# Strassen-style MLP of a two-layer streaming encoder: one block of down weights moved to other buffers, a tile of transposes moved, VectorE and ScalarE orders rewritten

## The reference

```
h = rms_norm(x, norm_mix);  proj = h @ w_in                  # q, k, v, u, gv
x = x + concat(window_attention(q, k, v, sinks), u * spatial_gating(gv)) @ w_o
h = rms_norm(x, norm_ffn)
x = x + square(relu(h @ w_up)) @ w_down                      # 1024 -> 4096 -> 1024
```

## Time and profile before

| | us |
|---|---|
| time, 3 runs: lowest, median, highest | 994.88, 997.0, 997.27 |
| the profiled execution's own time | 992.74 |
| its span, first to last instruction | 990.8 |
| PE busy (share of span) | 943.6 (95%) |
| DVE busy | 707.6 (71%) |
| ACT busy | 562.7 (57%) |
| POOL busy | 204.8 (21%) |

### The profile page before, as it was taken

The page is one execution under the profiler, slowest core; times in us unless marked ns, Lnnn a source line. Parts: engine busy times, 40 slices in busy tenths (PEclk is TensorE's granted clock), DMA queues, the critical chain, the costliest instruction groups (busy, mean ns, idle before and its releaser), DMA issues.

```text
span 990.8 us, 14055 instructions
## 1 busy us (share of the span) xinstructions
PE 943.6 (95%) x5632; PEld 828.1 (84%) x5632; DVE 707.6 (71%) x813; ACT 562.7 (57%) x843; POOL 204.8 (21%) x136
## 2 busy tenths in 40 slices
PE   8999998998999999999799999988989989998995
PEld 5888787987997998898688888888879879988984
DVE  5676436888787878868647761487876977878785
ACT  5556427674665574476455661657546735745753
POOL 2554223110110011001147424401101101100110
PEclk9999999999999999999899999989989999999998
DMA  8432050776577568474534213236838565775653
GB/s 292 136 103 84 22 170 1 192 153 208 140 170 204 133 177 204 121 215 85 190 102 160 78 62 83 87 85 173 193 105 236 122 192 135 168 207 128 173 105 128
DMA packets 40497, 141.76 MB, mean 143 GB/s; under 512 B 5616, under 2 KB 5744, under 8 KB 40432
## 3 DMA queue, kind: packets, MB, share of 16 engines
q1 hardware_dynamic: 28624, 98.32, 29.2%
q0 software_dynamic: 11520, 41.95, 23.9%
q10 hardware_dynamic: 288, 0.59, 0.2%
HBM read 138.74 MB, written 2.10 MB: 142 GB/s over the span
## 4 chain that ended last, share of the span: by engine, by line
PE 57%; DVE 19%; DMA 13%; ACT 5%; issue 5%; POOL 1%; SPq 0%; DVEq 0%; POOLq 0%; ACTq 0%
DMA raw<-weights_in 12%; PE bank L579 10%; PE bank L581 10%; PE bank L580 10%; DVE wlo L1289 9%; PE bank L576 7%; PE bank L578 7%; PE bank L577 7%; DVE flo L1553 3%; ACT whi L932 2%; DVE xt L1586 2%; DVE raw L1566 2%; PE bank L603 1%; PE bank L777 1%; DMA xt<-x_in 1%
## 5 line engine op out<-in xcount | busy, mean ns | idle before, releaser
L932 ACT ACTIVATE whi<-raw 128x1024 fp32r<-128x1024 f32 x268 | 279.5, 1056 | 174.4 <-DMA raw<-weights_in 88.5
L1289 DVE TENSOR_TENSOR wlo<-raw,whi 128x1024 fp32r<-128x1024 f32 x218 | 264.0, 1222 | 108.8 <-ACT whi L932 108.6
L579 PE MATMUL bank<-xhi,wlo 128*128 128x256 f32 (+1 forms) x672 | 211.2, 314 | 11.4 <-issue 8.9
L581 PE MATMUL bank<-xlo,whi 128*128 128x256 f32 (+1 forms) x672 | 209.2, 311 | 0.0
L580 PE MATMUL bank<-xhi,whi 128*128 128x256 f32 (+1 forms) x672 | 209.0, 311 | 0.0
L576 PE MATMUL bank<-wlo,fhi 128*128 128x512 f32 x448 | 179.2, 400 | 23.6 <-DVE xt L1586 20.1
L548 POOL DMA_DIRECT2D raw<-weights_in x80 | 69.4, 868 | 539.6 <-DVE raw L1566 333.1
L577 PE MATMUL bank<-whi,fhi 128*128 128x512 f32 x448 | 177.6, 396 | 0.0
L578 PE MATMUL bank<-whi,flo 128*128 128x512 f32 x448 | 177.5, 396 | 0.0
L535 POOL TENSOR_TENSOR wlo<-raw,whi 128x1024 fp32r<-128x1024 f32 x50 | 135.2, 2716 | 203.4 <-ACT whi L932 203.4
L579 PEld LDWEIGHTS bank<-xhi,wlo 128*128 128x128 f32 x672 | 130.4, 194 | 19.0 <-issue 12.5
(11 more groups left out here) (131 smaller groups left out, 1240.7 us busy)
## 6 DMA issues: line engine op xcount, KB each, us to landing
raw<-weights_in SPq DMA_DIRECT2D x172, 512.0 KB, 4.5
raw<-weights_in POOLq DMA_DIRECT2D x80, 512.0 KB, 6.2
xt<-x_in SPq DMA_DIRECT2D x4, 512.0 KB, 8.2
gbc<-gains_in SPq DMA_DIRECT2D x4, 512.0 KB, 4.5
out_t<-xt SPq DMA_DIRECT2D x3, 512.0 KB, 2.7
gbc<-gains_in ACTq DMA_DIRECT2D x1, 512.0 KB, 5.8
bias<-alibi_in SPq DMA_DIRECT2D x2, 256.0 KB, 7.3
wst<-ws_in SPq DMA_DIRECT2D x2, 256.0 KB, 6.9
```

Source lines behind the costliest of these rows:

```text
L579: pe.matmul(o, wlo[:, s, wc], hi[:, tokens], start=first, stop=False, skip_group_check=on_sum)
L581: return pe.matmul(o, whi[:, s, wc], lo[:, tokens], start=False, stop=last, skip_group_check=on_sum)
L932: act.activation(whi[:, n % SLOTS, :], raw_at(slot), ACT.Copy).then_inc(whi_ready, 1)
L1289: dve.tensor_tensor(wlo[:, n % SLOTS, :], raw_at(raw_slot(n)), whi[:, n % SLOTS, :], ALU.subtract) \
```

## The change

Four things change. First, the down phase's B22 for M3 goes into slots 2 and 3, when M4's lows are made, and no longer into M2's slots 4 and 5; the next quarter's M7, which also uses 2 and 3, is therefore loaded behind the lows of the down phase's M3, and stands last in SP's list. Second, M4's weight sum in the down phase is made by DVE from M2's block in slots 4 and 5, as in the up phase, and POOL's accumulating DMA for it goes. Third, the last tile of x is turned before the last quarter of product M1, not behind it. Fourth, the orders on DVE and ACT are new, in q0's up phase and in all down phases. The waits and counts follow. The diff, without the counting functions and the q > 0 branch of the up orders (which keeps its order):

```diff
@@ -71,11 +71,12 @@
 RAW_SLOTS = 6
 B11, B12, B21, B22 = range(4)
-PRODUCT_SLOT = (0, 4, 4, 2, 0, 2, 2)
+PRODUCT_SLOT = ((0, 4, 4, 2, 0, 2, 2), (0, 4, 2, 2, 0, 2, 2))
 PRODUCT_BLOCK = {M1: B11, M2: B21, M3: B22, M7: B22}
...
@@ -444,23 +443,24 @@
                 if pos >= 4:
                     wait_low(sp, nth(l, pos - 4))
                 elif l:
-                    wait_low(sp, nth(l - 1, group_pos(QUARTERS - 1, DOWN, M4 if pos < 2 else M5, pos % 2)))
+                    wait_low(sp, nth(l - 1, group_pos(QUARTERS - 1, DOWN, M3 if pos < 2 else M5, pos % 2)))
                 load(l * LAYER_ROWS + pos, mix_slot(pos))
             def load_block(l, q, ph, r, g):
-                before = divmod(phase(l, q, ph) - 1 - l * 2 * QUARTERS, 2)
                 if r == M3:
-                    wait_low(sp, nth(l, group_pos(q, ph, M2, g)))
+                    wait_low(sp, nth(l, group_pos(q, ph, M2 if ph == UP else M4, g)))
                     if ph == UP:
                         sp.wait_ge(weights_summed, summed_weights(l, q, UP, M4, g))
-                elif q or ph:
-                    wait_low(sp, nth(l, group_pos(*before, {M1: M5, M7: M4, M2: M3}[r], g)))
+                elif ph == DOWN:
+                    wait_low(sp, nth(l, group_pos(q, UP, {M1: M5, M7: M4, M2: M3}[r], g)))
+                elif q:
+                    wait_low(sp, nth(l, group_pos(q - 1, DOWN, {M1: M5, M7: M3, M2: M2}[r], g)))
                 elif r != M2:
-                    wait_low(sp, nth(l, MLP_POS - 4 + PRODUCT_SLOT[r] + g))
+                    wait_low(sp, nth(l, MLP_POS - 4 + PRODUCT_SLOT[UP][r] + g))
                 elif l:
-                    wait_low(sp, nth(l - 1, group_pos(QUARTERS - 1, DOWN, M3, g)))
-                load(block_row(l, q, ph, PRODUCT_BLOCK[r], g), PRODUCT_SLOT[r] + g)
+                    wait_low(sp, nth(l - 1, group_pos(QUARTERS - 1, DOWN, M2, g)))
+                load(block_row(l, q, ph, PRODUCT_BLOCK[r], g), PRODUCT_SLOT[ph][r] + g)
             def load_blocks(l, q, ph, r):
                 if q < QUARTERS:
@@ -507,10 +507,10 @@
                     load_blocks(l, q, UP, M3)
                     for r in (M7, M1, M2):
                         load_blocks(l, q, DOWN, r)
+                    load_blocks(l, q, DOWN, M3)
+                    load_blocks(l, q + 1, UP, M1)
+                    load_blocks(l, q + 1, UP, M2)
                     load_blocks(l, q + 1, UP, M7)
-                    load_blocks(l, q + 1, UP, M1)
-                    load_blocks(l, q, DOWN, M3)
-                    load_blocks(l, q + 1, UP, M2)
                 sp.wait_ge(w_used, nth(l, group_pos(QUARTERS - 1, UP, M3, 1)) + 1)
                 load_gain(2 * l + 2)
@@ -537,15 +537,13 @@
             def add_block(l, q, ph, r, g):
-                slot = PRODUCT_SLOT[r] + g
+                slot = PRODUCT_SLOT[ph][r] + g
                 if r == M7:
                     pool.wait_ge(raw_landed[slot], 16 * block_loads(l, q, ph, M7, g))
-                elif r == M5:
+                else:
                     wait_low(pool, nth(l, group_pos(q, ph, M1, g)))
                     pool.wait_ge(weights_summed, summed_weights(l, q, ph, M6, g))
-                else:
-                    wait_low(pool, nth(l, group_pos(q, ph, M6, g)))
-                pool.dma_start(raw_at(slot), weights[block_row(l, q, ph, B21 if r == M4 else B12, g)], accum_op=ALU.add) \
+                pool.dma_start(raw_at(slot), weights[block_row(l, q, ph, B12, g)], accum_op=ALU.add) \
                     .then_inc(sum_landed[slot], 16)
             def add_blocks(l, q, ph, r):
@@ -564,7 +562,6 @@
                     add_blocks(l, q, UP, M5)
                     add_blocks(l, q, DOWN, M7)
                     add_blocks(l, q, DOWN, M5)
-                    add_blocks(l, q, DOWN, M4)
         @block.tensor
         def _(pe):
@@ -897,11 +896,13 @@
                 pe.wait_ge(att_lo, l * 4 + 4)
                 mixed_tiles(l, lambda t: turn(2 * l + 1, t - 1) if t else None)
+                def turn_last(m):
+                    if m == PAIRS - 1:
+                        turn(2 * l + 1, NT - 1)
+
                 for q in range(QUARTERS):
                     for r in SEQUENCE[UP]:
-                        up_product(l, q, r)
-                        if q == 0 and r == M1:
-                            turn(2 * l + 1, NT - 1)
+                        up_product(l, q, r, turn_last if q == 0 and r == M1 else None)
                     for r in SEQUENCE[DOWN][:5]:
                         product(l, q, r)
                     if q < QUARTERS - 1:
...
@@ -1178,23 +1179,32 @@
                 def hi_down(q, r, g):
                     hi(group_pos(q, DOWN, r, g))
-                xs_high(0)
-                xs_high(1)
                 for q in range(QUARTERS):
-                    if q:
+                    if q == 0:
+                        xs_high(0)
+                        hi_up(q, M7, 1)
+                        copy_sum(q, M1, 0)
+                        copy_sum(q, M1, 1)
+                        hi_up(q, M6, 0)
+                        xs_high(1)
+                        hi_up(q, M6, 1)
+                        xs_high(2)
+                        hidden(q, M2, 0)
+                        hi_up(q, M4, 0)
+                        xs_high(3)
+                        hidden(q, M2, 1)
+                        hi_up(q, M4, 1)
...
                     copy_sum(q, M7, 0)
                     copy_sum(q, M7, 1)
                     factor_high(q, M1)
@@ -1219,15 +1229,15 @@
                     hi_down(q, M6, 1)
                     factor_high(q, M6)
                     factor_high(q, M4)
+                    factor_high(q, M5)
                     hi_down(q, M4, 0)
-                    factor_high(q, M5)
                     hi_down(q, M4, 1)
+                    factor_high(q, M2)
                     hi_down(q, M5, 0)
-                    factor_high(q, M2)
                     hi_down(q, M5, 1)
                     hi_down(q, M2, 0)
+                    hi_down(q, M2, 1)
                     factor_high(q, M3)
-                    hi_down(q, M2, 1)
                     hi_down(q, M3, 0)
                     hi_down(q, M3, 1)
                     if q < QUARTERS - 1:
...
+                def sum_m4(q, ph, g):
+
+                    wait_low(dve, nth(l, group_pos(q, ph, M6, g)))
+                    dve.wait_ge(raw_landed[PRODUCT_SLOT[ph][M2] + g], 16 * block_loads(l, q, ph, M2, g))
+                    t2 = raw_at(PRODUCT_SLOT[ph][M4] + g)
+                    dve.tensor_tensor(t2, t2, raw_at(PRODUCT_SLOT[ph][M2] + g), ALU.add).then_inc(weights_summed, 1)
...
@@ -1590,29 +1600,38 @@
                     add_product(q, r, 0)
                     add_product(q, r, 1)
-                xs_make(0)
-                xs_make(1)
-                xs_make(2)
-                xs_low(0)
-                xs_make(3)
-                xs_low(1)
                 for q in range(QUARTERS):
-                    low_up(q, M7, 0)
-                    if q:
+                    if q == 0:
+                        xs_make(0)
+                        low_up(q, M7, 0)
+                        xs_low(0)
+                        sum_m6(q, UP, 0)
+                        low_up(q, M7, 1)
+                        xs_make(1)
+                        xs_make(2)
+                        low_up(q, M6, 0)
+                        xs_low(1)
+                        sum_m6(q, UP, 1)
+                        low_up(q, M6, 1)
+                        sum_m4(q, UP, 0)
+                        up_sum(q, M2, 0)
+                        sum_m4(q, UP, 1)
+                        up_sum(q, M2, 1)
+                        xs_make(3)
+                        xs_low(2)
+                        xs_low(3)
...
                     low_up(q, M4, 0)
                     low_up(q, M4, 1)
                     factor_low(q, M1)
@@ -1638,19 +1657,21 @@
                     low_down(q, M6, 1)
                     add_both(q, M1)
                     factor_low(q, M6)
+                    sum_m4(q, DOWN, 0)
                     factor_low(q, M4)
+                    sum_m4(q, DOWN, 1)
+                    factor_low(q, M5)
                     low_down(q, M4, 0)
                     add_both(q, M7)
-                    factor_low(q, M5)
                     low_down(q, M4, 1)
+                    factor_low(q, M2)
                     low_down(q, M5, 0)
-                    factor_low(q, M2)
+                    add_both(q, M6)
                     low_down(q, M5, 1)
-                    add_both(q, M6)
                     low_down(q, M2, 0)
                     make(q, 3)
+                    low_down(q, M2, 1)
                     factor_low(q, M3)
-                    low_down(q, M2, 1)
                     add_both(q, M4)
                     low_down(q, M3, 0)
                     low_down(q, M3, 1)
```

(91 more changed lines are left out.)

18 lines of the change are left out of this document (7 added, 11 removed).

## The result

The changed kernel takes 964.4 us (median of 4 runs, 963.5 to 965.4), the kernel before, on the same chip, 995.9 (993.0 to 997.3). The ratio is 0.9687, with a 95% interval of 0.9661 to 0.9714; the prediction was 964.0 of 997.0, which is 0.9669. The profiled executions took 992.74 and 963.5 us, with spans of 990.8 and 961.7, so the traces have 29.1 us to explain.

A forecast was written before the change was run, and what follows sets the result against it. Bound: PE plus the one slot M3 shares with M2. Gains 22.0 + 7.6 - 1.0 + 4.1 = 32.7 us: 960.0 from the profiled 992.74, 964 from the median 997.0; 8-in-10 range 952 to 979.

The forecast's parts named there:

- The waits of the down phases: Eight down phases up to M3's start: of 23.62 us of PE waiting, 22.0 us would go.
- M5's add at M3: Down phase: the next thing late once M3's wait goes, with 0.5 to 1 us in hand in q0.
- the 1.6 us set aside: Waiting left in down phases: 0.6 us twice in last quarters, 0.2 us twice before M4 in q0.
- The half clock behind them: Lower PE clock behind the down-phase waits goes with them: 7.6 us, not counting 1.72 at the end.
- The change of layers and the start of the MLP: Next norm's third tile late for PE after layer 0, -1.0 us; new start of the MLP gains 4.1 us.
- this clock loss goes with it: 3.3: Layer 1, up M3's start: M5's bank sum 2.4 us sooner, 1.7 us of half clock gone; 3.3 us gained.
- VectorE's sum costs nothing while 0.5 to 1 us is left: Down phases: 16 sums, 2.45 us a phase, fit DVE's idle 2.87 and 1.67 us, costing nothing on the path.
- Rival (a): DVE becomes the bound in the down phases, giving all 19.6 us back: 984 us; chance 0.08.
- The load of M7 in the next quarter: M7's load, now behind M3's lows, has 7 us in hand at the medians: no cost.
- The other end, -42 us: Next quarter's M7 late at the maximum load times, 6 us missing: -42 us for six transitions.
- The middle quarters: Sign: quarters in the middle last 78.7 to 79.2 us in both layers; wrong at 80 or more.
- DVE's busy time: Sign: DVE's busy time, with the 16 new sums, is up by 19 to 20 us.

The follow-up runs named there:

- down_only: Changed kernel with the old start of the MLP (turn after M1, old orders in q0's up phase): 965.4 us, ratio 0.9677 to the kernel before.
- slot_poolsum: Changed kernel with M4's down-phase sum again by POOL's accumulating load, M3 still in M4's slots: 959.1 us, ratio 0.9599 to the kernel before.
- sum_only: Kernel before with only M4's down-phase weight sum moved to VectorE, M3 still in M2's slots: 1003.9 us, ratio 1.006.
- Swap: Changed kernel with M5's first bank sum ahead of down M1's first low in q0, ACT's steps to match: 963.8 us, ratio 0.9644 to the kernel before.
- swap2: Changed kernel with both of up M5's bank sums ahead of both of down M1's lows in q0: 964.1 us, ratio 0.9649 to the kernel before.
- fill: Changed kernel with 20 unused matmuls on PE ahead of up M4 in q0: 963.8 us, ratio 0.9655 to the kernel before.
- start_only: Kernel before with only the new start of the MLP (turn inside M1, new orders in q0's up phase): 995.3 us, ratio 0.9998.
- extra2: Changed kernel with two unused 400-column DVE additions more in each down phase: 972.6 us, ratio 0.9732 to the kernel before.
- extra4: Changed kernel with four unused 400-column DVE additions more in each down phase: 986.0 us, ratio 0.9873 to the kernel before.

## Why the prediction was right, and where it was not

1. **The waits of the down phases** (22.0 us): 22.6 by the ledger. That M3 starts with M2's end is shown of the slot and the new down orders together: down_only and slot_poolsum have both and no wait worth the name before M3, sum_only has neither and keeps it. No run has the orders without the slot, nor the slot with the old orders. By q0's rows they alone could bring M2's lows, and the load behind them, about 1.1 us forward, since the split of M5's factor moves into DVE's 1.67 us of idleness; that is an estimate of up to 9 of the 22.6 us, and how much of the gain is the slot's alone stays open. What was due next was also right, M5's add at M3 with 0.9 us in hand (0.5 to 1 predicted), and M7's add before M4, where PE waits 0.64 and 0.30 in q0 (0.2 each predicted). Against the 1.6 us set aside, 2.1 came.
2. **The half clock behind them** (7.6 us): M3's products gave 9.1, of which the last one's 10.02 - 8.41 = 1.6 went into the end, 1.6 longer, as said. Net 7.5.
3. **The change of layers and the start of the MLP** (-1.0 + 4.1 = 3.1 us): measured -1.5 + 0.5 = -1.0. This is the mis-sized term of the sum, 4.1 us off. The sentence that failed is "this clock loss goes with it: 3.3", with the unsaid one that layer 0 keeps its 0.8 up to the end of the phase; how the 3.3 comes out of the 2.4 and 1.7 beside it, the text doesn't show either. I had M4's start right to 0.1 us, and stopped there. M3 needs M5's bank sums, which stand behind the lows of down M1, whose second load took 11.4 us in place of 7.5. In layer 1 M3 waits 2.44 us at 671.04, and the lower clock that I let go is there again (0.67 over 5.16 us). In the second profiled execution of the changed kernel it is not: the waits are 1.10 and 0.68 and the clock 1.00, and the span is 962.2 all the same. Swap, swap2 and fill show that this region absorbs what is gained ahead of it; start_only shows no gain from the new start that can be told.
4. **VectorE's sum costs nothing while 0.5 to 1 us is left**: wrong in size. The changed kernel is slower than with POOL's sum, by 4.5 us in the traces (2.6 in the down phases, the rest as above). The two were not timed beside each other; their ratios to the kernel before are 0.9659 to 0.9687 and 0.9599. I had weighed the sum against 2.87 + 1.67 us of idleness, but the 2.87 were idle because M3 was late, and went with the wait, and of the 1.67 the new order fills a part with the split of M5's factor. The forecast of 22.0 left 1.6 us of waiting; I did not see that it was the price of the sum and could be had back. Rival (a), DVE as the bound at 984, did not happen, but extra2 and extra4, at 973 and 986, show that it begins less than 1 us per phase away.
5. **The load of M7 in the next quarter**: no wait, as forecast. The other end, -42 us, doesn't follow from its terms: 260.9 against the 254.4 at which the load is needed is 6.5 us, 39 for six. POOL's issues are where they were, changed kernel:

```profile
L546 POOL DMA_DIRECT2D raw<-weights_in x64: 865/865/1002, 129.6 to 917.1; - x64
...
DMA to landing us min/median/max: 5.3/5.8/10.6
```

POOL's median issue is 865 ns beside 16 more two-input operations of DVE. The Trainium skill, "GPSIMD Engine Reference", its table of specifications, has such instructions contend with GpSimd; no issue here shows it, the longest taking 1002 ns and 1000 before.

Of the signs, the granted clock of 1.00 in the down phases and the waits before up M4 (5.25 us) and M7 (none) came as said. The middle quarters, at 78.42 us, came 0.3 below the range. DVE's busy time rose by 15.6 us and not by 19 to 20: that forecast took each sum at its full 1.225 us, though operations in a row start 1.13 to 1.14 apart.

The sum was 32.7 us, and the trace has 29.1: 22.6 + 7.5 - 1.0. The prediction of 964 came from the median of 997.0, 4.3 above the profiled execution; by the profiled executions alone it said 960.0 for 963.5. The median hit by more than it had earned: runs of the kernel before, at 996 to 1000 from batch to batch, move by as much as the miss.

## What to carry to other kernels

Idle time of an engine that lies behind the wait you remove is no room for new work: lay the order out without the wait, and count what is left. When a buffer's reuse holds a load back, another slot, with orders laid out for it, is worth the wait and the lower clock behind it; work moved to the busier engine for it should be tried both ways. At a start where several engines hand over to each other, follow the new order up to the last consumer and not only to the first wait that moves.

## What the runs showed of the hardware

- A 512 KB load takes 3.3 us at best, but near 10 at the median where eight were issued from 184 to 200 us in the changed kernel, and 6.5 where the kernel before issued its eight there.
- In the changed kernel both waits of 5.2 us were followed by a lower clock (185.45: a mean of 0.61 over 6.85 us; 655.62: 0.80 over 6.88), while one of 1.54 was not at 201.08, and one of 2.44 was at 671.04. The length of the wait doesn't settle it: in down_only one of 3.12 us at 202.78 was followed by 5.22 us at 1.00. Twenty matmuls in the wait kept it at 1.00.
- Operations of DVE of 1.22 us follow each other at 1.13 to 1.14, and time that two share counts once. 16 sums at 1.14 would be 18.2 us; DVE's busy time rose by 15.6. That operations which had stood alone now overlap too would explain the rest, but was not measured.
- Sixteen accumulating loads of 512 KB, 6.0 us to landing at the median of all 80, cost this kernel less than 16 sums of 1.22 us on a DVE with no idle time: with the loads back the span is 957.2 us for 961.7.
